# One core of a hybrid decoder layer: values computed in feature layout and transposed, an earlier query tile, and denominators in two fp32r parts

## The chip, the core and the metric

The kernel runs on one core of one Trainium2 chip. The metric is the device time of one execution in microseconds (us), and lower is better. In this kernel TensorE (PE in the profile) does the matrix products. ScalarE (ACT) and VectorE (DVE) carry results out of PSUM and do the elementwise work. GpSimd (POOL) splits every weight tile into two parts, and the SyncE queue (SP) loads the weights.

## What is computed

One layer over 528 tokens (16 meta tokens and a sequence of 512), model width 1024. One input projection feeds three parallel mixers (GLA, a sparse attention, mLSTM), whose outputs are gated and summed, and an MLP follows. The change concerns the values of GLA and of mLSTM (four heads of 256 columns each), the normaliser of mLSTM, and the first products of the sparse attention's query path.

```python
z = xn @ p["w_in"] + p["b_in"]          # 528 x 1024 times 1024 x N_COLS
# GLA, per chunk:   o = (q * exp(G)) @ S + A @ v
# mLSTM, per chunk:
num = w_inter[..., None] * jnp.einsum("bhtk,bhkv->bhtv", q, Cs) + jnp.einsum("bhts,bhsv->bhtv", P, v)
den = w_inter * jnp.einsum("bhtk,bhk->bht", q, ns) + jnp.sum(P, axis=-1)
h = num / jnp.maximum(jnp.abs(den), jnp.exp(-m))[..., None]
```

## The kernel before

**Precision.** Large products are made of three fp32r products: high part by high part, low by high, high by low. The input is held as `xh` and `xl`, features on partitions. SP loads a chunk of 1024 x 128 weights into `wraw`, and POOL writes its rounded part `whi` and the rest `wlo` (`hi_done` and `split_done` count them). Three raw and four split chunks are held.

**The stream of products.** `plan()` lists the tiles that TensorE computes in order. Each goes into one of two accumulators `GP[0]` and `GP[1]`, by turns. `gemm(name)` waits until its accumulator has been emptied (`gfree`) and its chunks are split, runs the tile's products and increments `gemm_done`. `evacuated(name)` waits until the result of a tile has been carried out. A tile of kind F (a feature tile) has 128 output features on partitions. With `both=True` it covers all 528 tokens in two halves of 264, so 8 x 3 x 2 = 48 products. The order on each engine is written out by hand, and an engine that waits holds back all that stands behind it.

**Values.** A head's values are needed with tokens on partitions. They are computed so: the input is the stationary operand and two weight chunks are streamed, 256 columns wide. Tiles `...A` and `...B` (kind V) take two token tiles of 128 each, 48 products a tile. A third tile `...M` (kinds VM and VT) computes 16 meta or last tokens, 16 products with 32 stationary columns (`xm`, L1879 and L1880). VectorE adds the bias from a broadcast row `vb` as it empties them (`values`, L1392 and L1397) into `vh` and `vm`.

**mLSTM, head h, on TensorE.** The query tile of the next head in two halves with `squares` between them, `scores` 0 and 1, the key tile, `scores` 2 and 3, values A of the next head, then `recalled` (the weighted values, L2291 and L2292). Then the denominators: sums of the weights over keys, by a matrix of ones in fp32, in two products of 112 and 400 columns (L2322, L2324). Then values B and M.

**mLSTM on the other engines.** VectorE multiplies the scores by decays (L1688), adds them up for the denominators (`weight_sums`, L1696 to L1700), runs the next head's two convolutions (`conv`, L1658 and L1660), and finishes the head. ScalarE runs the exponentials. After the last scores it takes one sigmoid for each convolution (L996), the output gate (L1039), loads the table for ln and exp (`lnexp`, L638), and squares the head's output (L1049).

```python
if more:
    conv_sig(h + 1, 1)
lnexp()
head_squares(h)
```

**The start.** The query path has two tiles, `cq0` and `cq1`, each computed in two halves of 256 tokens (`half`). TensorE begins with the high parts of `cq0`, as soon as two input tiles are there.

Of the kernel before, what the change touches and what calls it, by code (L numbers as in the profile page):

```python
# [24 lines left out]
D = 1024  # L25
# [44 lines left out]
def _rows():  # L70
    at = 0
    for name, n, src in [
        ("gq", 4, "b_in"), ("gk", 4, "b_in"), ("gr", 8, "b_in"), ("cq", 2, "b_in"), ("ckv", 1, "b_in"),
        ("ik", 1, "b_in"), ("mq", 4, "b_in"), ("mk", 4, "b_in"), ("mo", 8, "b_in"), ("gate", 24, "b_in"),
        ("a2", 4, "b_gla_a"), ("hg", 2, "g_gla_head"),
        ("hm", 2, "g_ml_head"), ("dq", 2, "g_dsa_q"), ("dkv", 1, "g_dsa_kv"), ("ig", 1, "idx_ln_g"),
        ("ib", 1, "idx_ln_b"), ("fb", 1, "ml_f_bias"), ("cv", 32, "ml_conv"),
    ]:
        ROWS[name] = at
        ROW_LIST.append((name, n, src))  # L80
        at += n
    return at
# [6 lines left out]
JOINED = {"gq": 8, "cq": 3, "mq": 8}  # L89
FOLLOWS = ("gk", "ckv", "mk")  # L90
# [21 lines left out]
NROWDMA = 22  # L112
# [22 lines left out]
def plan():  # L135
# [27 lines left out]
    def values(name, c0):  # L163
        c = [chunk("w_in", c0, P), chunk("w_in", c0 + P, P)]
        assert c[0] % 2 == 0
        tile(name + "A", c, 0, kind="V", off=0)
        tile(name + "B", c, 0, kind="V", off=2)
        tile(name + "M", c, 2, kind="VT" if name[0] == "m" else "VM")

    def pad():  # L170
        if len(chunks) % 2:
            chunks.append(None)
# [8 lines left out]
    state["slot"] ^= 1  # L181
# [42 lines left out]
    def all_values(name, c0):  # L224
        pad()
        values(name, c0)

    gla(0)
    all_values("gv0", C_GV)
    for h in range(HEADS):  # L230
        if h + 1 < HEADS:
            gla(h + 1)
        else:
            gates("ta", C_GATE, 0, 2)
        pairs("gr", C_GR, h)
        if h + 1 < HEADS:
            all_values(f"gv{h + 1}", C_GV + (h + 1) * DV)
# [6 lines left out]
    all_values("mv0", C_MV)  # L244
    for h in range(HEADS):
        if h + 1 < HEADS:
            feature(f"mq{h + 1}", "w_in", C_MQ + (h + 1) * DK, both=True)
            feature(f"mk{h + 1}", "w_in", C_MK + (h + 1) * DK, both=True)
        else:
            gates("tc", C_GATE + 2 * D, 0, 2)  # L250
        if h + 1 < HEADS:
            all_values(f"mv{h + 1}", C_MV + (h + 1) * DV)
# [37 lines left out]
def build(nc, a, line, scratch, rows, out):  # L290
# [3 lines left out]
    with ctx:  # L294
# [6 lines left out]
        def region(offset, specs):  # L301
# [23 lines left out]
        xm = sb("xm", [P, KT, 2 * META], F32R)  # L325
# [44 lines left out]
        (sgate, gtmp, vb, qh, ATm, kh, vh, vm, AT, sqo, rso, on, km) = region(AO, [  # L370
            ("sgate", [P, 2, SEQ], FP32), ("gtmp", [P, 2, SEQ], FP32), ("vb", [P, D], FP32),
# [3 lines left out]
        BO = AO + (2 * SEQ * 2 + D + 2 * SEQ + 2 * ALL + 2 * QT * DV + 2 * DV + QT * SEQ + SEQ + 2 * SEQ + SEQ + 2 * SEQ + 2 * P) * 4  # L375
# [7 lines left out]
        (zc, cv, sgc, lf_, bcum_, M_, uT, uTt, fbias_, um_, Mb, Md, Wd, Mt, Wt, ATt, later_t) = region(BO, [  # L383
# [5 lines left out]
            ("later_t", [2 * META, META], FP32)])  # L389
        (onesr,) = region(BO + (6 * ALL + 4 * SEQ + 144) * 4, [("onesr", [P, P], F32R)])  # L390
        later = ATm
        (sqr,) = region(AO + (7 * SEQ + D + 2 * ALL + 2 * QT * DV + 2 * DV + QT * SEQ) * 4, [("sqr", [P, 2, SEQ], F32R)])
        (qg,) = region(AO + (4 * SEQ + D) * 4, [("qg", [P, 2, QT, P + P // 2], FP32)])
# [17 lines left out]
        def gate_store(m):  # L411

            return [vh[:, 0, 0:2, :].rearrange("p a b -> p (a b)"), vh[:, 0, 2:4, :].rearrange("p a b -> p (a b)"),
                    kh[:, 0, 0:SEQ], qh[:, 0, :], vb[:, 0:SEQ], vb[:, SEQ:D], AT[:, 0, :], AT[:, 1, :]][m]
# [61 lines left out]
        ld_v, zpad, cv_ok, cs_ok, qk_ok = sem("ld_v"), sem("zpad"), sem("cv_ok"), sem("cs_ok"), sem("qk_ok")  # L476
# [3 lines left out]
        xt_ok, ml_c = sem("xt_ok"), sem("ml_consts")  # L480
# [147 lines left out]
        def _(act):  # L628
# [41 lines left out]
            def input_high(t):  # L670

                if t == QT:
# [3 lines left out]
                    act.wait_ge(xh_ok, KT + 1)  # L676
                    nc.scalar.activation(xm[:, :, 0:META], xh[:, :, 0:META].bitcast(FP32), ACT.Copy).then_inc(xh_ok, 1)
# [21 lines left out]
            for k in range(2):  # L699
                nc.scalar.activation(cq[:, k, :], ready(f"cq{k}")[:, 0:SEQ], ACT.Identity, bias=cc("cq", k)).then_inc(gfree[tl[f"cq{k}"].slot], 1)  # L700
# [144 lines left out]
            act.dma_start(vb[:, :], a["b_in"][0:1, C_GV:C_GV + D].broadcast_to([P, D])).then_inc(ld_a, 16)  # L845
# [81 lines left out]

            gate_of(0)
            for h in range(HEADS):
                last = h == HEADS - 1  # L930
                level(h, 0)
                if h:
                    squared(h - 1)
                level(h, 1)
# [20 lines left out]
                off_out(h)  # L955
                sigmoids(h)
                if last:

                    whole("gv3M")
# [20 lines left out]
            act.dma_start(vb[:, :], a["b_in"][0:1, C_MV:C_MV + D].broadcast_to([P, D])).then_inc(ld_v, 16)  # L980
# [64 lines left out]
            fetch_maxima(0)  # L1045
            def head_squares(h):
# [10 lines left out]
            for h in range(HEADS):  # L1057
# [15 lines left out]
                floor_of(h)  # L1073
                if more:
# [10 lines left out]
                if not more:  # L1085
                    gate_in("tc", 16, 2)
                head_squares(h)
            gate_in("tc", 16, 3)
            whole("mv3M")
# [88 lines left out]
        def _(dve):  # L1178
# [45 lines left out]
            def input_low(t):  # L1224
                if t == QT:
# [3 lines left out]
                    dve.wait_ge(xl_ok, KT + 1)  # L1229
                    nc.vector.tensor_copy(xm[:, :, META:2 * META], xl[:, :, 0:META].bitcast(FP32)).then_inc(xl_ok, 1)  # L1230
# [155 lines left out]
            dve.wait_ge(ld_a, 48)  # L1386

            def values(name, h, part):
                if part < 2:
                    t = tl[f"{name}{h}{'AB'[part]}"]  # L1390
                    ps = ready(f"{name}{h}{'AB'[part]}")
                    tt(vh[:, h % 2, 2 * part:2 * part + 2, :], ps[:, 0:2 * DV].rearrange("p (t n) -> p t n", t=2),  # L1392
                       vb[:, h * DV:(h + 1) * DV].unsqueeze(1).broadcast_to([P, 2, DV]), ALU.add).then_inc(gfree[t.slot], 1)
                    return
                ps = ready(f"{name}{h}M")
                dve.wait_ge(f16_ok, 2)
                stt(vm[0:2 * META, h % 2, :], vb[0:2 * META, h * DV:(h + 1) * DV], first16[:, :], ps[0:2 * META, 0:DV], ALU.mult, ALU.add).then_inc(gfree[tl[f"{name}{h}M"].slot], 1)  # L1397
# [91 lines left out]
            def off(h):  # L1489
# [6 lines left out]
                if h + 1 < HEADS:  # L1496
                    values("gv", h + 1, 0)
# [55 lines left out]
            for part in range(3):  # L1553
                values("gv", 0, part)
            for h in range(HEADS):
# [33 lines left out]
                if more:  # L1589
                    values("gv", h + 1, 1)  # L1590
                    values("gv", h + 1, 2)
# [5 lines left out]
            def gate_rows_of(m):  # L1597
# [18 lines left out]
                if m == 3:  # L1616
                    dve.wait_ge(gemm_done, tl["gv3M"].val)
                    nc.vector.tensor_copy(xm[:, :, 0:META], xh[:, :, SEQ:ALL].bitcast(FP32)).then_inc(xt_ok, 1)
                    nc.vector.tensor_copy(xm[:, :, META:2 * META], xl[:, :, SEQ:ALL].bitcast(FP32)).then_inc(xt_ok, 1)
# [4 lines left out]
                if m == 5:  # L1624
                    nc.vector.tensor_copy(later[:, 0:DIAG[0]], later_bigT[:, META:P])
# [75 lines left out]

            def denominator(h):
# [25 lines left out]
            dve.wait_ge(ld_v, 16)  # L1728
            for part in range(3):
                values("mv", 0, part)  # L1730
            for h in range(HEADS):
                more = h + 1 < HEADS
                masked(h)
                if h:
                    head_scaled(h - 1)
                for j in range(2):
# [6 lines left out]
                if more:  # L1743
                    conv(h + 1, 0)
                if h:
                    low_parts(8, h - 1)
                if more:
                    conv_mul(h + 1, 0)
                    conv(h + 1, 1)
                    values("mv", h + 1, 0)  # L1750
# [3 lines left out]
                if more:  # L1754
                    for part in range(1, 3):
                        values("mv", h + 1, part)
# [84 lines left out]
        def _(pe):  # L1841
# [9 lines left out]
            def gemm(name, part=None):  # L1851
# [22 lines left out]
                elif t.kind in ("V", "VM", "VT"):  # L1874
                    s0 = chunks[t.chunks[0]]["hl"]
                    if t.kind != "V":
                        for k in range(KT):
                            w = slice(k * P, (k + 1) * P)
                            mm(ps[0:2 * META, 0:DV], xm[:, k, :], whi[:, s0:s0 + 2, w], start=(k == 0), stop=False)  # L1879
                            ins = mm(ps[0:2 * META, 0:DV], xm[:, k, :], wlo[:, s0:s0 + 2, w], start=False, stop=(k == KT - 1))  # L1880
                    tokens = [] if t.kind != "V" else [0, 1] if part is None else [part]
                    first = 0 if name[0] == "m" else META
                    for i in tokens:
                        tok = slice(first + (t.off + i) * P, first + (t.off + i + 1) * P)
                        o_ = ps[:, i * DV:(i + 1) * DV]
                        for k in range(KT):
                            for p_, (at_, wt) in enumerate([(xh, whi), (xh, wlo), (xl, whi)]):
                                ins = mm(o_, at_[:, k, tok], wt[:, s0:s0 + 2, k * P:(k + 1) * P],  # L1888
# [564 lines left out]
```

## Time and profile before

| what | value |
|---|---|
| time, median of 3 runs | 1264.04 us (1263.27 to 1264.69) |
| the profiled execution, its time | 1264.5 us |
| its span in the trace | 1261.8 us |
| PE busy | 1253.5 us, 99% |
| POOL, DVE, ACT busy | 772.8, 629.2, 392.9 us |
| chain that ended last | PE 99% |

The chain that ended last is followed back from the last instruction. Here nearly all of it is TensorE's own work, one product behind the other. Matmuls are pipelined, so a row shows longer durations than what a product costs in a stream. The cost is the distance from one start to the next.

### The profile page before, as it was taken

Reading aid. Unit: us, or ns where it says so; the run is one execution under the profiler, and the core shown is the slowest. Engines: PE = TensorE matmul, PEld = TensorE weight load, DVE = VectorE, ACT = ScalarE, POOL = GpSimd, SP = SyncE. Lnnn points to the kernel's source line nnn. Section 1 sums busy time; section 2 is a strip of 40 time slices with the busy share of each in tenths; the row PEclk is TensorE's granted clock in tenths of the full one; section 3 lists DMA queues with packets and bytes.
Section 4 is the critical chain, followed back from the end, with each engine's and each line's share of the span. In section 5 each row is a group of like instructions: output and inputs, shape, how many; then the busy total and the mean of one; then the engine's idle time right before and its main releaser. Section 6 shows DMA issues by size and latency. Waiting matters only on the chain.

```text
span 1261.8 us, 17439 instructions
## 1 busy us (share of the span) xinstructions
PE 1253.5 (99%) x6561; PEld 1029.2 (82%) x6564; DVE 629.2 (50%) x1115; ACT 392.9 (31%) x810; POOL 772.8 (61%) x914
## 2 busy tenths in 40 slices
PE   9999999999999999999999999999999999999998
PEld 8866887677899899888899987887888888888886
DVE  4368888642276886835447773342511112333434
ACT  5343565533023323333024343312511111221322
POOL 8746430125584753758775556784876677888882
PEclk9999999999999999999999999999999999999999
DMA  7847200223231322322433333522233333232321
GB/s 177 241 122 224 68 1 26 68 67 94 71 97 51 84 62 56 84 68 84 117 110 78 86 97 100 188 95 84 84 101 100 85 100 105 96 100 84 101 84 67
DMA packets 167433, 120.08 MB, mean 95 GB/s; under 512 B 11367, under 2 KB 145613, under 8 KB 167350
## 3 DMA queue, kind: packets, MB, share of 16 engines
q1 hardware_dynamic: 160612, 107.79, 29.7%
q10 hardware_dynamic: 6738, 11.18, 2.7%
q8 instruction: 52, 0.85, 0.3%
q14 instruction: 31, 0.25, 0.1%
HBM read 114.71 MB, written 9.62 MB: 99 GB/s over the span
## 4 chain that ended last, share of the span: by engine, by line
PE 99%; DVE 0%; ACT 0%; issue 0%; DVEq 0%; ACTq 0%
PE GP L1873 46%; PE GP L1909 9%; PE PA L1909 9%; PE GP L1888 7%; PE GP L1870 6%; PE PA L2073 3%; PE GP L2135 3%; PE PA L2173 1%; PE PA L2110 1%; PE PA L2291 1%; PE GP L2366 1%; PE GP L1954 1%; PE PA L2043 1%; PE PA L2283 1%; PE PA L2074 1%; PE GP L1880 1%
## 5 line engine op out<-in xcount | busy, mean ns | idle before, releaser
L623 POOL TENSOR_TENSOR wlo<-wraw,whi 128x256 fp32r<-128x256 f32 x708 | 564.7, 828 | 14.7
L619 POOL TENSOR_SCALAR whi<-wraw 128x1024 fp32r<-128x1024 f32 x177 | 201.1, 1136 | 449.9 <-PE GP L1873 227.2
L1873 PE MATMUL GP<-xh,whi 128*128 128x512 f32 x352 | 144.8, 411 | 0.0
L1873 PE MATMUL GP<-xh,wlo 128*128 128x512 f32 x352 | 139.1, 395 | 0.0
L1873 PE MATMUL GP<-xl,whi 128*128 128x512 f32 x352 | 138.8, 394 | 0.0
L1815 DVE TENSOR_TENSOR ul<-U,uh 128x512 fp32r<-128x512 f32 x64 | 65.2, 1054 | 109.5 <-ACT uh L1157 109.5
L1873 PE MATMUL GP<-nh,whi 128*128 128x512 f32 x240 | 95.1, 396 | 0.0
L1873 PE MATMUL GP<-nl,whi 128*128 128x512 f32 x240 | 95.1, 396 | 0.0
L1873 PE MATMUL GP<-nh,wlo 128*128 128x512 f32 x240 | 95.1, 396 | 0.0
L1819 DVE SCALAR_TENSOR_TENSOR U<-GP,rrow 128x512 f32<-128x512 f32 x32 | 22.1, 692 | 141.7 <-PE GP L1873 140.3
L1873 PEld LDWEIGHTS GP<-xh,whi 128*128 128x128 f32 x352 | 66.2, 188 | 16.0 <-issue 1.5
L1873 PEld LDWEIGHTS GP<-xh,wlo 128*128 128x128 f32 x352 | 66.1, 188 | 15.2
L1873 PEld LDWEIGHTS GP<-xl,whi 128*128 128x128 f32 x352 | 66.3, 188 | 14.3 <-issue 0.5
L1157 ACT ACTIVATE uh<-U 128x512 fp32r<-128x512 f32 x64 | 37.2, 625 | 129.0 <-PE PA L1909 70.4
L1873 PE MATMUL GP<-yh,whi 128*128 128x512 f32 x192 | 76.3, 397 | 0.0
L1873 PE MATMUL GP<-yl,whi 128*128 128x512 f32 x192 | 76.1, 396 | 0.0
L1873 PE MATMUL GP<-yh,wlo 128*128 128x512 f32 x192 | 76.1, 396 | 0.0
L1888 PE MATMUL GP<-whi,xh 128*128 128x256 f32 x256 | 74.6, 292 | 0.2 <-DVE kh L1403 0.2
L1888 PE MATMUL GP<-wlo,xh 128*128 128x256 f32 x256 | 71.9, 281 | 0.0
L1888 PE MATMUL GP<-whi,xl 128*128 128x256 f32 x256 | 71.7, 280 | 0.0
L1161 ACT ACTIVATE U<-U 128x512 f32<-128x512 f32 x32 | 20.2, 632 | 152.9 <-DVE U L1819 152.9
L1873 PEld LDWEIGHTS GP<-nh,wlo 128*128 128x128 f32 x240 | 45.2, 188 | 11.0
(426 smaller groups left out, 2771.5 us busy)
## 6 DMA issues: line engine op xcount, KB each, us to landing
wraw<-in_w_in SPq DMA_DIRECT2D x75, 512.0 KB, 3.9
wraw<-in_w_up SPq DMA_DIRECT2D x32, 512.0 KB, 4.0
wraw<-in_w_down SPq DMA_DIRECT2D x32, 512.0 KB, 3.5
line_rows<-bias_line SPq DMA_DIRECT2D x8, 655.0 KB, 5.1
table<-line_rows SPq DMA_DIRECT2D x4, 1024.0 KB, 5.6
wraw<-in_w_br_dsa SPq DMA_DIRECT2D x8, 512.0 KB, 4.2
wraw<-in_w_br_gla SPq DMA_DIRECT2D x8, 512.0 KB, 3.9
wraw<-in_w_br_ml SPq DMA_DIRECT2D x8, 512.0 KB, 4.0
```

The lines of the kernel that those rows point to most:

```text
L619: nc.gpsimd.tensor_scalar(hi, src, 1.0, 1.0, ALU.mult, ALU.mult).then_inc(hi_done, 1)
L623: part = nc.gpsimd.tensor_tensor(lo[:, at:to], src[:, at:to], hi[:, at:to].bitcast(FP32), ALU.subtract)
L1157: nc.scalar.activation(uh[:, k % 4, :], U[:, k % FT, :], ACT.Copy).then_inc(uh_ok, 1)
L1161: nc.scalar.activation(U[:, m, :], U[:, m, :], ACT.Square).then_inc(U_ok, 1)
L1815: tt(ul[:, k % 4, :], U[:, k % FT, :], uh[:, k % 4, :].bitcast(FP32), ALU.subtract).then_inc(ul_ok, 1)
L1819: stt(U[:, m, :], ps[:, 0:SEQ], 0.0, rrow[:, :], ALU.max, ALU.mult).then_inc(gfree[tl[f"up{m}"].slot], 1)
L1870: ins = mm(ps[0:t.m, b * SEQ:b * SEQ + HALF], wt[:, s0, w], hx[:, k, b * HALF:(b + 1) * HALF], start=st, stop=sp_)
L1873: ins = mm(ps[0:t.m, 0:SEQ], wt[:, s0, w], av, start=st, stop=sp_)
L1888: ins = mm(o_, at_[:, k, tok], wt[:, s0:s0 + 2, k * P:(k + 1) * P], start=(k == 0 and p_ == 0), stop=(k == KT - 1 and p_ == 2))
L1909: ins = mm(accumulators(name, hf, i), av[:, i * P:(i + 1) * P], wt[:, c["hl"], k * SEQ:(k + 1) * SEQ], start=(n == 0 and k == 0 and p_ == ...
L2073: mm(bank(v % 2)[0:r, 0:w], qlat[:, h, TILE_AT[i]:TILE_AT[i + 1]], kvT[:, 0:w], start=True, stop=False)
L2135: ins = mm(pairs_of(o_, g), kvn[:, j, :], pairs_of(PT[:, g % 2, j, :], g), start=(j == 0), stop=(j == i))
```

## The change

Values become feature tiles. A head has two (`gv00`, `gv01`; `mv00`, `mv01`), each of 48 products of 264 columns, like keys. ScalarE empties such a tile into `vT` with the bias added (`value_in`). A new tile of kind T (`...T0`, `...T1`) then transposes `vT` on TensorE against the identity: four transposes of 128 tokens and one of 16. VectorE copies it to `vh` and `vm`; T1 of GLA goes by ScalarE (`values_copied`). The tiles M, the buffer `xm` and the broadcast rows `vb` go. The bias rows are loaded with the other rows (22 loads become 20). `cq1`'s first high half is issued before `cq0`'s second half, in the second bank of the same accumulator. The mLSTM denominators are rounded by ScalarE (`sum_hi`), the rest is taken by VectorE (`weight_rest`, `sum_lo`), and TensorE sums both by two fp32r products of 512 columns.

```diff
+    def value(name, c0, h, v):
+        feature(f"{name}{h}{v}", "w_in", c0 + (2 * h + v) * P, both=True)
+            def value_in(name, h, v):
+                if h:
+                    act.wait_ge(gemm_done, tl[f"{name}{h - 1}T{v}"].val)
+                t = tl[f"{name}{h}{v}"]
+                nc.scalar.activation(two(vT[:, v, :]), halves(ready(f"{name}{h}{v}")), ACT.Identity,
+                                     bias=cc(name, 2 * h + v)).then_inc(gfree[t.slot], 1)
...
@@ ScalarE, head h of mLSTM
                 floor_of(h)
+                act.wait_ge(sum_w, h + 1)
+                for c, s_ in WSUM:
+                    ins = nc.scalar.activation(Wr[:, 1, c], s_[:, c], ACT.Copy)
+                ins.then_inc(sum_hi, 1)
...
                 if more:
                     conv_sig(h + 1, 1)
                 lnexp()
-                if not more:
+                if more:
+                    value_in("mv", h + 1, 0)
+                else:
                     gate_in("tc", 16, 2)
                 head_squares(h)
+                if more:
+                    value_in("mv", h + 1, 1)
...
@@ VectorE
+            def weight_rest(h):
+                dve.wait_ge(sum_hi, h + 1)
+                for c, s_ in WSUM:
+                    ins = tt(Wr[:, 0, c], s_[:, c], Wr[:, 1, c].bitcast(FP32), ALU.subtract)
+                ins.then_inc(sum_lo, 1)
...
                 weight_sums(h)
                 if more:
                     conv(h + 1, 0)
+                weight_rest(h)
...
@@ TensorE
+                elif t.kind == "T":
+                    v, first = int(name[4]), 0 if name[0] == "m" else META
+                    few = slice(SEQ, ALL) if name[0] == "m" else slice(0, META)
+                    evacuated(name[0:3] + name[4])
+                    for i in range(QT):
+                        nc.tensor.transpose(ps[:, i * P:(i + 1) * P], vT[:, v, first + i * P:first + (i + 1) * P], ident[:, :])
+                    ins = nc.tensor.transpose(ps[0:META, SEQ:SEQ + P], vT[:, v, few], ident[:, :])
...
-                nxt("mvA")
+                nxt("mv0")
...
-                mm(bank(3)[:, 0:FROM[1]], ones[:, :], AT[:, 0, 0:FROM[1]], start=True, stop=True)
-                pe.wait_ge(sum_w, h + 1)
-                mm(bank(3)[:, FROM[1]:SEQ], ones[:, :], Wd[:, 0, FROM[1]:SEQ], start=True, stop=True).then_inc(av_ps, 1)
-                nxt("mvB")
-                nxt("mvM")
+                pe.wait_ge(sum_lo, h + 1)
+                mm(bank(3), onesr[:, :], Wr[:, 1, :], start=True, stop=False)
+                mm(bank(3), onesr[:, :], Wr[:, 0, :], start=False, stop=True).then_inc(av_ps, 1)
+                nxt("mvT0")
+                nxt("mv1")
...
@@ TensorE, start
             half("cq0", 0, low, False, True)
+            pe.wait_ge(hi_done, 2)
+            half("cq1", 0, high, True, False)
             pe.wait_ge(xl_ok, KT)
             half("cq0", 1, high, True, False)
```

TensorE at the end of mLSTM's head 0, before: the last of the weighted values, the denominators, and the first products of values B of head 1.

```order
L2291 MATMUL PA<-AT,vh 128x144
L2292 MATMUL PA<-ATt,vm 128x16
L2322 MATMUL PA<-AT,ones 128x112
L2324 MATMUL PA<-Wd,ones 128x400
L1888 MATMUL GP<-whi,xh 128x256
L1888 MATMUL GP<-wlo,xh 128x256
```

And now:

```order
L2305 MATMUL PA<-AT,vh 128x144
L2306 MATMUL PA<-ATt,vm 128x16
L2338 MATMUL PA<-Wd_r,onesr 128x512
L2339 MATMUL PA<-Wd_r,onesr 128x512
L1901 MATMUL GP<-ident,vT 128x128 x4
L1902 MATMUL GP<-ident,vT 16x128
L1892 MATMUL GP<-xh,whi 128x264 x2
```

The tile `mv1T0` (`ident,vT`) stands between the denominators and the next large tile, where products of the large tile followed at once.

ScalarE at the same place, before: the two sigmoids of head 1's convolutions (`sgc`), the output gate, the table load, the squares of head 0.

```order
L996 ACTIVATE sgc<-cv 128x528
L988 ACTIVATE zc<-GP,col 128x528
L1039 ACTIVATE sgate<-sgate 128x512 x2
L996 ACTIVATE sgc<-cv 128x528
L638 ACT_TABLE_LOAD
L1049 ACTIVATE sqo<-PA 128x1024
L1051 ACTIVATE gtmp<-gtmp 128x512
```

And now:

```order
L1018 ACTIVATE sgc<-cv 128x528
L1010 ACTIVATE zc<-GP,col 128x528
L1061 ACTIVATE sgate<-sgate 128x512 x2
L1018 ACTIVATE sgc<-cv 128x528
L645 ACT_TABLE_LOAD
L937 ACTIVATE vT<-GP,col 128x528
L1073 ACTIVATE sqo<-PA 128x1024
L1075 ACTIVATE gtmp<-gtmp 128x512
L937 ACTIVATE vT<-GP,col 128x528
```

The copy `vT` that `mv1T0` transposes is made behind the second sigmoid and the table load; the second copy follows the squares.

## Rows read from the trace of the kernel before

**Rows 1.** The page, busy time of TensorE, and its granted clock in 40 slices.
```profile
PE 1253.5 (99%) x6561; PEld 1029.2 (82%) x6564; DVE 629.2 (50%) x1115; ACT 392.9 (31%) x810; POOL 772.8 (61%) x914
...
PEclk9999999999999999999999999999999999999999
```

**Rows 2.** Waits of TensorE: releaser, us in total, times, longest us.
```profile
PE GP L1954 <- DVE xl L1235: 0.6, 1, 0.6
```

**Rows 3.** Instructions of L1888, window 340 to 375 us: duration min/median/max, first and last start.
```profile
L1888 PE MATMUL GP<-whi,xh x32: 279/280/387, 347.5 to 358.5; 128*128 128x256 f32 x32
```

**Rows 4.** Timeline of TensorE, tile M of GLA's head 0: start, us, line.
```profile
358.89 0.28 PE L1879 MATMUL GP<-whi,xm 128*32 128x256 f32 x1
...
360.73 0.40 PE L1873 MATMUL GP<-xh,whi 128*128 128x512 f32 x1
```

**Rows 5.** Timeline of TensorE, first half of a query tile in mLSTM, then `squares`.
```profile
680.94 0.40 PE L1870 MATMUL GP<-xh,whi 128*128 128x264 f32 x2
...
683.85 0.40 PE L2195 MATMUL PA<-sqr,onesr 128*128 128x512 f32 x1
...
684.32 0.40 PE L1870 MATMUL GP<-xh,whi 128*128 128x264 f32 x2
```

**Rows 6.** Timeline of TensorE, four transposes between fp32r products, GLA's head 0.
```profile
395.62 0.28 PE L1888 MATMUL GP<-whi,xl 128*128 128x256 f32 x1
...
395.88 0.30 PE L2235 MATMUL PA<-ident,km 128*128 128x128 f32 x1
...
396.02 0.49 PE L2237 MATMUL PA<-ident,KHt 128*128 128x128 f32 x3
...
396.27 0.36 PE L1888 MATMUL GP<-whi,xh 128*128 128x256 f32 x1
```

**Rows 7.** Timeline of TensorE, mLSTM's head 1 from its last scores to values B.
```profile
695.43 0.36 PE L1888 MATMUL GP<-whi,xh 128*128 128x256 f32 x1
...
701.17 0.59 PE L2291 MATMUL PA<-AT,vh 128*128 128x512 f32 x1
...
706.00 0.45 PE L2322 MATMUL PA<-AT,ones 128*128 128x112 f32 x2
...
707.10 0.28 PE L1888 MATMUL GP<-wlo,xh 128*128 128x256 f32 x1
```

**Rows 8.** Timeline of VectorE in the same stretch.
```profile
696.03 0.58 DVE L1696 TENSOR_TENSOR Wd<-AT 128x400 f32<-128x400 f32 x1
...
698.30 0.59 DVE L1700 TENSOR_TENSOR Wd<-Wd,ATt 16x16 f32<-16x16 f32 x1
...
699.33 2.74 DVE L1660 SCALAR_TENSOR_TENSOR cv<-zc,col,cv 128x528 f32<-128x528 f32 x3
```

**Rows 9.** Timeline of ScalarE in the same stretch.
```profile
702.66 0.68 ACT L988 ACTIVATE zc<-GP,col 128x528 f32<-128x528 f32 x1
...
706.95 0.65 ACT L996 ACTIVATE sgc<-cv 128x528 f32<-128x528 f32 x1 [2.58 <-DVE cv L1660]
707.62 1.28 ACT L638 ACT_TABLE_LOAD   x1
708.91 1.03 ACT L1049 ACTIVATE sqo<-PA 128x1024 f32<-128x1024 f32 x1
```

**Rows 10.** Timeline at the end of head 0: denominators on TensorE, table load on ScalarE.
```profile
672.45 0.45 PE L2322 MATMUL PA<-AT,ones 128*128 128x112 f32 x2
...
673.65 1.28 ACT L638 ACT_TABLE_LOAD   x1
```

**Rows 11.** Timeline of ScalarE in GLA, from the off-diagonal copies to the next head.
```profile
396.55 0.60 ACT L879 ACTIVATE AT<-PA 128x512 f32<-128x512 f32 x1 [5.85 <-PE PA L2237]
...
399.63 1.28 ACT L638 ACT_TABLE_LOAD   x1
```

**Rows 12.** Timeline of weight loads at the start, before the first real products.
```profile
1.24 4.90 PEld L1930 LDWEIGHTS PA<-ones 128*128 128x128 f32 x26 [1.24 <-DVE ones L1202]
...
7.89 0.86 PEld L1930 LDWEIGHTS PA<-ones 128*128 128x128 f32 x7 [0.24 <-issue]
```

More of the change, by code:

```diff
@@ L161, in feature, with turned @@
         tile(name, [c], 1, kind="F", m=m, kt=kt, both=both, rhs=rhs, off=0, width=m)
[L163 to L172, printed above, removed]
+    def turned(name, v):
+        tile(f"{name}T{v}", [], 0, kind="T")
     feature("cq0", "w_in", C_CQ)
+    state["slot"] = 0
     feature("cq1", "w_in", C_CQ + P)
+    tiles["cq1"].need = 0
     feature("ik", "w_in", None, both=True)
@@ L222, in gates @@
             feature(f"{name}{m}", "w_in", c0 + m * P)
-    def all_values(name, c0):
-        pad()
-        values(name, c0)
+    def value(name, c0, h, v):
+        feature(f"{name}{h}{v}", "w_in", c0 + (2 * h + v) * P, both=True)
     gla(0)
-    all_values("gv0", C_GV)
+    value("gv", C_GV, 0, 0)
+    value("gv", C_GV, 0, 1)
+    turned("gv0", 0)
+    turned("gv0", 1)
     for h in range(HEADS):
@@ L699, in _ @@
             for k in range(2):
-                nc.scalar.activation(cq[:, k, :], ready(f"cq{k}")[:, 0:SEQ], ACT.Identity, bias=cc("cq", k)).then_inc(gfree[tl[f"cq{k}"].slot], 1)
+                nc.scalar.activation(cq[:, k, :], ready(f"cq{k}")[:, k * SEQ:(k + 1) * SEQ], ACT.Identity, bias=cc("cq", k)).then_inc(gfree[tl[f"cq{k}"].slot], 1)
             whole("cq0")
@@ L955, in _ @@
                 off_out(h)
+                if not last:
+                    value_in("gv", h + 1, 0)
                 sigmoids(h)
+                if not last:
+                    value_in("gv", h + 1, 1)
                 if last:
-                    whole("gv3M")
                     gate_in("ta", 0, 3)
@@ L1084, in _ @@
                 lnexp()
-                if not more:
+                if more:
+                    value_in("mv", h + 1, 0)
+                else:
                     gate_in("tc", 16, 2)
                 head_squares(h)
+                if more:
+                    value_in("mv", h + 1, 1)
             gate_in("tc", 16, 3)
-            whole("mv3M")
             gate_in("tc", 16, 4)
@@ L1385, in _, with values @@
             nc.vector.tensor_copy(small[0:32, HALF:ALL], small[96:P, HALF:ALL]).then_inc(gla_c, 1)
[L1386 to L1397, printed above, removed]
+            def values(name, h, v):
+                ps, c = ready(f"{name}{h}T{v}"), slice(v * P, (v + 1) * P)
+                nc.vector.tensor_copy(vh[:, h % 2, :, c], ps[:, 0:SEQ].rearrange("p (t n) -> p t n", t=QT))
+                nc.vector.tensor_copy(vm[0:META, h % 2, c], ps[0:META, SEQ:SEQ + P]).then_inc(gfree[tl[f"{name}{h}T{v}"].slot], 1)
             def q_in(h):
@@ L1552, in _ @@
             forget_sums(0)
-            for part in range(3):
-                values("gv", 0, part)
+            values("gv", 0, 0)
             for h in range(HEADS):
@@ L1727, in _ @@
             dve.wait_ge(ml_c, 2)
-            dve.wait_ge(ld_v, 16)
-            for part in range(3):
-                values("mv", 0, part)
+            values("mv", 0, 0)
             for h in range(HEADS):
@@ L1735, in _ @@
                     head_scaled(h - 1)
+                values("mv", h, 1)
                 for j in range(2):
@@ L1754, in _ @@
                 if more:
-                    for part in range(1, 3):
-                        values("mv", h + 1, part)
+                    values("mv", h + 1, 0)
             head_scaled(HEADS - 1)
@@ L1873, in gemm @@
                                 ins = mm(ps[0:t.m, 0:SEQ], wt[:, s0, w], av, start=st, stop=sp_)
[L1874 to L1888, printed above, removed]
-                                         start=(k == 0 and p_ == 0), stop=(k == KT - 1 and p_ == 2))
+                elif t.kind == "T":
[5 more added lines that the diff above has]
+                    ins = nc.tensor.transpose(ps[0:META, SEQ:SEQ + P], vT[:, v, few], ident[:, :])
                 else:
@@ L1988, in _ @@
             ins.then_inc(xt_ps, 1)
-            pe.wait_ge(hi_done, 2)
-            half("cq1", 0, high, True, False)
             half("cq1", 1, high, False, False)
@@ L2268, in _ @@
             gemm("mk0")
-            for nm in ("mv0A", "mv0B"):
+            for nm in ("mv00", "mv01", "mv0T0"):
                 gemm(nm)
-            pe.wait_ge(xt_ok, 2)
-            gemm("mv0M")
             pe.wait_ge(M_ok, 1)
```

112 lines of the change are left out of this document (61 added, 51 removed).

## The prediction

> **What bounds the kernel now.** I read the page first. TensorE is busy for 1253.5 of 1261.8 us and its granted clock is 9 tenths or more in each of 40 slices [rows 1], so no stretch leaves TensorE waiting for long, and the chain that ended last is TensorE. The list of its waits then tells how thin the rest is: the one wait that this change touches is 0.6 us for the low part of the input [rows 2]. A change to such a kernel has two prices. What it takes from or adds to TensorE's own stream counts in full. And each result that a product now needs from another engine must be there when TensorE arrives, since no idle time exists to absorb it. So I price the products by the distance of their starts, and then follow the three engines at each new wait.
>
> **TensorE's stream.** Eight heads (four of GLA, four of mLSTM) change their values.
> (a) Tile M goes: 16 products from 358.89 to the next tile at 360.73, 1.84 us [rows 4]. Eight times: -14.7 us.
> (b) The 96 large products of a head stay 96, but stream 264 columns for 256. L1888 shows 32 of every third product from 347.5 to 358.5, which is 11.0 us for 93 products, 0.1183 each [rows 3]. The 24 products of a half query tile take 680.94 to 683.85, 0.1213 each [rows 5]. 768 x 0.0030 = +2.3 us.
> (c) Ten transposes a head, in 16 tiles of five. In the trace four stand between products: the product at 395.62 would have been followed at 395.74, and the next came at 396.27 [rows 6]. So four cost 0.53 us with the change of kind, five 0.66. Where a neighbour is fp32 already (the weighted values of GLA, the scores) the change of kind is paid before, so I take 0.60 a tile, 16 tiles: +9.6 us. Bounds: three transposes alone take 396.02 to 396.27, so five take at least 0.42 (6.7 us in all), and at most 0.72 (11.5).
> (d) The denominators: from 706.00 to where the stream is regular again, 707.10 less one step of 0.12, is 0.98 us [rows 7]. Two fp32r products of 512 columns with ones are in the trace, 683.85 to 684.32, 0.47 us [rows 5]. Four heads: -2.0 us.
> (e) The start: `cq1`'s 16 high products fill the wait of 0.6 us for `xl` [rows 2]. Their weights come second from the split, and nothing waits behind them for longer. -0.6 us.
> The stream's sum is -5.4 us. The loads of the bias rows lie beside other work and cost nothing.
>
> **The new waits.** A T tile needs `vT` from ScalarE, so each of the 16 has to be checked.
> GLA, T0: ScalarE is free behind the copy at 396.55, so from about 397.2 [rows 11], and the first value tile is ready by then. The product at 396.27 begins a half of the second value tile [rows 6]; with the other half that is 48 x 0.1213 = 5.8 us, so TensorE comes to T0 after 402. No wait. T1: ScalarE is done with the sigmoids and the load at 400.9 [rows 11], waits for the second value tile and copies it while TensorE runs T0 and the weighted values. No wait. Only in the first head does T1 come directly behind T0, and likewise mLSTM's first query tile behind `mv0T0`: each copy of 0.7 us is covered by 0.6 us of transposes, which leaves 0.2 us or so each, +0.4 us.
> mLSTM, T1: it comes after a whole query tile. No wait.
> mLSTM, T0 of heads 1, 2 and 3 is the place that decides. TensorE comes to it directly behind the denominators, but ScalarE makes its input behind the second convolution's sigmoid and the table load. I follow head 1 of the trace, where T0 of head 2 will stand.
> TensorE: the value tile begins at 695.43 and takes 5.82 now, the weighted values take 701.17 to 706.00, 4.83, the denominators 0.47 [rows 7]. It arrives at 706.55.
> ScalarE: the sigmoid at 706.95 waits for VectorE's `cv` [rows 9]. VectorE's chain begins with the last scores just before 695.43 and runs without a gap (the sums end at 698.9, the first convolution at 702.07 [rows 8]), and the change puts `weight_rest` into it: 400 columns by 0.58 [rows 8], 112 columns by about 0.25, together 0.83. So the sigmoid begins at 707.78, the load 0.67 later, the copy 1.29 after that (706.95, 707.62, 708.91 in rows 9) at 709.74. The copy of 128x528 from PSUM is 0.68 [rows 9], its signal some 0.1: T0 can begin at 710.5. TensorE stands for 3.9 us.
> Head 2 of the trace repeats head 1, 33.55 us later, so T0 of head 3 waits 3.9 too. In head 0 the table load stands at 673.65, and the denominators began at 672.45 [rows 10]. There VectorE had to wait 0.7 us for the first sigmoid, so `weight_rest` hides in it but for 0.1: copy from 675.05, T0 from 675.8. TensorE arrives at 672.45 + 0.09 + 0.47 = 673.0, and waits 2.8 us.
> Together 10.6 us. These can't be recovered later in the head: T0 must be emptied and the next tile computed before the scores, and the scores restart the same chain, so the wait comes back in each head.
> What else is new on ScalarE, the two rounding copies, lies in a gap: the sums end at 698.9, the copies need 0.3 and 0.6, the table load 1.28, and the first sigmoid is due at 702.1 when its convolution ends. `weight_rest` ends near 702.9, and the denominators need it at 706.1, so 3.2 us are left.
>
> **A rule and a row.** Behind the load at 707.62 the next activation starts at 708.91, and before it the sigmoid of 0.65 begins at 706.95, so the switch costs 1.29 us and nothing else fits in [rows 9]. The Trainium skill (ScalarE: Activation LUTs, What ACT_TABLE_LOAD costs) adds a drain of some 1380 ns to each load. By that, T0 would be 1.4 us later in three heads and the sum would be 4.1 us higher; the row decides against it.
>
> **The sum.** -5.4 + 0.4 + 10.6 = +5.6 us on a span of 1261.8 us, so 1267.4. The profiled execution took 1264.5 us, 0.5 above the median, so I work from the median of 1264.04: 1269.7 us, +0.44%.
>
> **Rivals.**
> *The copy is in time* (faster). If ScalarE had `vT` by 706.5, the waits would vanish, and 1264.04 - 5.4 + 0.4 = 1259.0 us stays. It turns at 3.9 us: the sigmoid would have to start at 703.9 and not 707.8. For it: VectorE's other work in the head gets less (its bias additions go). Against it: those stood behind the convolutions or before the scores, and the sigmoid's wait is for `cv` itself [rows 9].
> *The wait is cut to a half*, if the convolution starts earlier or the stream before T0 is longer than I priced it: 1262 to 1266 us.
> *The clock falls in the waits.* The granted clock stays full through the trace [rows 1], but the only wait of TensorE inside the work that is listed here is 0.6 us long [rows 2], and waits of 3.9 us are new. The first loads of all, after idle time, come every 0.19 us (26 in 4.90), later ones of the same form every 0.12 (7 in 0.86) [rows 12], though the granted clock of that slice shows nothing of it. If TensorE wakes up so behind a wait, with the clock at 1.2 for a while and not at 2.4 GHz, the price is about what the start paid: 26 x 0.065 = 1.7 us a wait. In two or three heads that gives 1273.1 to 1274.8. The Trainium skill (TensorE: Matmul & The Clock Gate, HAM oscillation) says that idle gaps between bursts of products bring the slow clock back. No row here has such a gap, so this stays a rival with a chance of 0.22.
> *Another new wait*, as `sum_lo` coming late or T1 of GLA held by ScalarE's queue: 3.2 us of slack would have to go; a few us, 1272 to 1275.
>
> **How the numbers follow.** Forecast as summed 0.58, clock 0.22, another wait 0.05, cut wait 0.07, copy in time 0.08. Bounds of the forecast alone: transposes -2.9 to +1.9, `weight_rest` and the copy together 0.3 less or 0.5 more in each of three heads, 264 columns 1 us either way: 1266.3 to 1273. To hold 8 in 10 it needs part of the clock case and no faster one: 1265.5 to 1274.5. No change is within 0.2% (2.5 us, about what a measurement of this kernel tells from none), 1261.5 to 1266.6. Faster 0.09, same 0.06, slower 0.85.
>
> **What the changed profile would show.** Waits of TensorE for ScalarE's `vT` at the transposes, three times, 2.8, 3.9 and 3.9 us, and the sum of its idle time up by 10 us. No rows of `xm`; 80 transposes of `vT` at 0.60 us per five. The two denominator products 0.47 us apart from start to T0's earliest place. A wait at `xl` of under 0.1 us at the start. `sum_lo` not among TensorE's waits. The granted clock below 1 behind a wait would speak for the clock. Wrong it would be if `cv` is ready some 3 us earlier relative to the last scores, or if T0 waits nowhere.

## The result and the profile after

The changed kernel takes 1282.33 us (median of 4 runs, 1282.08 to 1282.79) against 1263.76 us for the kernel before (4 runs, 1263.27 to 1264.69). The ratio is 1.0145, 95% interval 1.0132 to 1.0158: slower by 18.6 us. The forecast was slower by 5.6, 1269.7 us, with a range up to 1274.5. The direction is right and the size is not.

The profiled span is 1280.9 us, 19.1 more than before. This is the page of the changed kernel, which answers to [rows 1]; the second line is TensorE's busy share in tenths, the third its granted clock.

```profile
PE 1255.3 (98%) x6505; PEld 1031.0 (80%) x6508; DVE 621.5 (49%) x1120; ACT 408.1 (32%) x841; POOL 773.9 (60%) x914
...
PE   9999999999999999999998889999999999999998
...
PEclk9999999999999999999998889999999999999999
```

Three slices, 672 to 769 us, are below 9 in both rows; T0 of mLSTM's heads 1, 2 and 3 lies in them. The list of TensorE's waits says for what (releaser, us in total, times, longest us); `xl` of [rows 2] is gone from it.

```profile
PE GP L1901 <- ACT vT L937: 17.4, 4, 6.2
...
PE GP L1892 <- ACT vT L937: 0.4, 1, 0.4
```

L1901 is the transpose, L937 ScalarE's copy. Of the 17.4 us, 0.34 is T1 of GLA's first head. The rest is T0 of mLSTM's heads 1, 2 and 3: 4.62, 6.21 and 6.19 us. TensorE's timeline (start, us, line), first the transposes of `mv0T1`, then head 2, to compare with [rows 7]:

```profile
652.04 0.60 PE L1901 MATMUL GP<-ident,vT 128*128 128x128 f32 x4
...
711.41 0.48 PE L2338 MATMUL PA<-Wd_r,onesr 128*128 128x512 f32 x1
711.73 0.39 PE L2339 MATMUL PA<-Wd_r,onesr 128*128 128x512 f32 x1
718.32 1.09 PE L1901 MATMUL GP<-ident,vT 128*128 128x128 f32 x4 [6.21 <-ACT vT L937]
...
729.74 0.40 PE L2209 MATMUL PA<-sqr,onesr 128*128 128x512 f32 x1
```

The wait stands at the place that the prediction named. Two things are off. It is 6.2 us and not 3.9. And the transposes take 1.09 us for four, where four took 0.60 at 652.04: the clock is low. ScalarE there, the rows that answer to [rows 9]:

```profile
715.52 0.64 ACT L1018 ACTIVATE sgc<-cv 128x528 f32<-128x528 f32 x1 [5.92 <-DVE cv L1677]
716.18 1.28 ACT L645 ACT_TABLE_LOAD   x1
717.48 0.70 ACT L937 ACTIVATE vT<-GP,col 128x528 f32<-128x528 f32 x1
```

Sigmoid, load, copy follow each other as worked out, 1.96 us from the first start to the third. It is the sigmoid that starts late, and it waits for VectorE. VectorE's rows, for [rows 8], and below them GpSimd's:

```profile
707.21 1.11 DVE L1723 TENSOR_TENSOR Wd_r<-AT,Wd_r 128x112 fp32r<-128x112 f32 x1
708.24 0.56 DVE L1723 TENSOR_TENSOR Wd_r<-Wd,Wd_r 128x400 fp32r<-128x400 f32 x1
708.73 2.35 DVE L1562 TENSOR_TENSOR yl<-on,yh 128x512 fp32r<-128x512 f32 x2
711.00 1.21 DVE L1688 SCALAR_TENSOR_TENSOR qh<-cv,sgc 128x512 f32<-128x512 f32 x1
712.34 0.74 DVE L1675 TENSOR_SCALAR cv<-zc,col 128x528 f32<-128x528 f32 x1
713.11 2.38 DVE L1677 SCALAR_TENSOR_TENSOR cv<-zc,col,cv 128x528 f32<-128x528 f32 x3
```

```profile
706.91 1.29 POOL L626 TENSOR_SCALAR whi<-wraw 128x1024 fp32r<-128x1024 f32 x1 [1.78 <-PE GP L1892]
708.28 4.50 POOL L630 TENSOR_TENSOR wlo<-wraw,whi 128x256 fp32r<-128x256 f32 x4
```

112 columns take 1.11 us and 400 columns 0.56. All that is slow begins before 712.8, while GpSimd splits a weight chunk. In the kernel before GpSimd did nothing in this stretch: both value chunks were held until tile M (L1880) was done. Its row there, with the idle time ahead of it:

```profile
714.82 1.86 POOL L619 TENSOR_SCALAR whi<-wraw 128x1024 fp32r<-128x1024 f32 x1 [14.92 <-PE GP L1880]
```

Now a chunk ends with its own tile.

The granted clock and the load of the DMA engines in the same stretch, by windows (busy us and count for PE, PEld, DVE, ACT and POOL, then the granted clock, DMA share, GB/s):

```profile
709.00:711.00 2.00, 2.00 (x7) 1.18 (x8) 2.00 (x3) 0.60 (x2) 2.00 (x3) 1.00 0.01 4
713.00:715.00 2.00, 0.00 (x0) 0.00 (x0) 1.89 (x4) 0.00 (x0) 0.00 (x0) 1.00 0.48 104
715.00:717.00 2.00, 0.00 (x0) 0.00 (x0) 1.26 (x3) 1.46 (x2) 0.00 (x0) 0.76 0.53 158
717.00:719.00 2.00, 0.68 (x4) 0.71 (x5) 1.41 (x3) 1.99 (x4) 0.00 (x0) 0.50 0.00 0
719.00:721.00 2.00, 2.00 (x11) 1.92 (x11) 1.81 (x3) 0.61 (x2) 0.00 (x0) 0.50 0.00 0
721.00:723.00 2.00, 2.00 (x11) 2.00 (x11) 1.97 (x5) 0.00 (x0) 0.00 (x0) 0.53 0.00 0
723.00:725.00 2.00, 2.00 (x19) 2.00 (x18) 0.20 (x2) 0.00 (x0) 0.00 (x0) 1.00 0.00 0
```

TensorE is idle from 712 to 718.3, its clock falls to 0.50, the 1.2 GHz level, and comes back after 722. A window of 2 us touches 11 products at the low level and 19 at the full one. DMA is not what slows VectorE: from 709 to 711, where two steps of `yl` take 2.35 us, it moves 4 GB/s.

From these rows came the theory for the experiments: -5.4 us of stream as forecast, +17.8 us of waits, and +6 to 7 us of work at the low clock, together +19. The rivals are named with each run.

### The profile page after: what moved, and what is told of

Same layout as the page of the kernel before. It is cut to its first block, busy times and chain, and to the rows that moved or that the text cites. A ratio compares the mean times of both kernels' runs of the same rounds, so it can differ in the third digit from the quotient of the medians.

```text
span 1280.9 us, 17359 instructions
## 1 busy us (share of the span) xinstructions
PE 1255.3 (98%) x6505; PEld 1031.0 (80%) x6508; DVE 621.5 (49%) x1120; ACT 408.1 (32%) x841; POOL 773.9 (60%) x914
## 4 chain that ended last, share of the span: by engine, by line
PE 94%; DVE 3%; ACT 1%; issue 1%; POOL 1%; DVEq 0%; ACTq 0%; POOLq 0%
PE GP L1895 45%; PE GP L1892 13%; PE GP L1922 9%; PE PA L1922 9%; PE PA L2087 3%; PE GP L2149 3%; PE PA L2187 1%; PE PA L2124 1%; DVE cv L1677 1%; PE GP L2381 1%; PE GP L1968 1%; PE PA L2057 1%; PE PA L2297 1%; PE GP L1901 1%; PE PA L2088 1%
## 5 line engine op out<-in xcount | busy, mean ns | idle before, releaser
L630 POOL TENSOR_TENSOR wlo<-wraw,whi 128x256 fp32r<-128x256 f32 x708 | 577.7, 846 | 14.8
L626 POOL TENSOR_SCALAR whi<-wraw 128x1024 fp32r<-128x1024 f32 x177 | 188.7, 1066 | 467.9 <-PE GP L1895 248.1
L1892 PE MATMUL GP<-xh,whi 128*128 128x264 f32 x480 | 104.3, 299 | 0.7 <-ACT vT L937 0.4
L1892 PE MATMUL GP<-xl,whi 128*128 128x264 f32 x480 | 99.3, 289 | 0.0
L1892 PE MATMUL GP<-xh,wlo 128*128 128x264 f32 x480 | 98.8, 288 | 0.0
L1892 PEld LDWEIGHTS GP<-xh,whi 128*128 128x128 f32 x480 | 77.5, 194 | 4.5 <-issue 2.1
L1895 PEld LDWEIGHTS GP<-xh,whi 128*128 128x128 f32 x352 | 66.2, 188 | 16.6 <-issue 1.9
L1895 PEld LDWEIGHTS GP<-xh,wlo 128*128 128x128 f32 x352 | 66.1, 188 | 15.5
L1895 PEld LDWEIGHTS GP<-xl,whi 128*128 128x128 f32 x352 | 66.3, 188 | 14.1 <-issue 0.5
L1892 PEld LDWEIGHTS GP<-xl,whi 128*128 128x128 f32 x480 | 76.6, 193 | 0.0
L1892 PEld LDWEIGHTS GP<-xh,wlo 128*128 128x128 f32 x480 | 76.2, 193 | 0.0
```

Source lines behind the costliest of these rows:

```text
L626: nc.gpsimd.tensor_scalar(hi, src, 1.0, 1.0, ALU.mult, ALU.mult).then_inc(hi_done, 1)
L630: part = nc.gpsimd.tensor_tensor(lo[:, at:to], src[:, at:to], hi[:, at:to].bitcast(FP32), ALU.subtract)
L1892: ins = mm(ps[0:t.m, b * SEQ:b * SEQ + HALF], wt[:, s0, w], hx[:, k, b * HALF:(b + 1) * HALF], start=st, stop=sp_)
L1895: ins = mm(ps[0:t.m, 0:SEQ], wt[:, s0, w], av, start=st, stop=sp_)
```

## First experiments: the wait, its length, the clock, the denominators

All are edits of the changed kernel. The kernel before took 1263.64 us beside them (7 runs).

**The copy earlier.** ScalarE's queue is the nearest suspect: the copy stands behind a sigmoid that waits.

```diff
                     conv_in(h + 1, 1)
+                    value_in("mv", h + 1, 0)
...
                 lnexp()
-                if more:
-                    value_in("mv", h + 1, 0)
-                else:
+                if not more:
```

> The changed kernel, but ScalarE makes the copy vT of the next head's first value tile right behind the copy of its key tile (conv_in), ahead of the output gate, the second sigmoid and the table load; nothing else moves. Theory from the trace of the changed kernel: its excess of 19 us over the kernel before is -5.4 us of stream, +17.8 us of waits for vT (4.6, 6.2 and 6.2 at T0 of heads 1 to 3, 0.4 twice at the first heads) and +6 to 7 us of slow clock behind the three long waits. Then the three long waits go and with them the slow clock: 1264.0 - 5.4 + 0.8 = 1259.4 us, up to 1262 if the keys of the next head (kh, km) are now late where they were not. Rival, the copy is late for another reason than the queue behind the sigmoid and the load (ScalarE itself is full, or the accumulator is): the waits stay within 1 us of what they are, 1281 to 1283 us. Rival, the waits go but the clock stays low, since something else than the wait brings it down: 1265 to 1267 us.

It took 1278.99 us, ratio 1.012 (1.0105 to 1.0135). None of the three cases came. The long waits at T0 are gone, yet almost all the time stays. The waits of this kernel:

```profile
PE GP L1891 <- DVE vm L1419: 8.1, 2, 5.2
PE GP L1894 <- DVE vm L1419: 5.2, 1, 5.2
```

L1891 and L1894 are the large products of the tile behind `mv1`: the next query tile, or the gate tile in the last head. It goes into the accumulator that T0 has filled, and VectorE empties that in `values`, behind the denominator and the sums of squares. TensorE passes T0 on time and stands one tile later, 2.8, 5.2 and 5.2 us. The clock falls again (0.50 from 718 to 724). So a tile of kind T has two dependencies one behind the other, input and emptying, and both hung on VectorE's chain. My theory was incomplete, and the theory that the head follows VectorE's chain was not in my list.

**GpSimd idle beside the chain.** The chunk of the first value tile is held until the second is computed.

```diff
             value("mv", C_MV, h + 1, 1)
+            chunks[tiles[f"mv{h + 1}0"].chunks[0]]["end"] = tiles[f"mv{h + 1}1"].val
```

> The changed kernel, but the weight chunk of the first value tile of mLSTM's heads 1 to 3 counts as used until the second value tile is computed, as two chunks were held before; so GpSimd has no chunk to split while VectorE runs the convolutions. Theory: VectorE's instructions in the chain to T0 take longer beside GpSimd's split (a copy for the low part 1.11 us against an estimate of 0.58 from its neighbour of the same size, qh 1.2 us against 0.7, yl 2.35 us for two against 1.3), and this makes the waits at T0 4.6, 6.2 and 6.2 us where 2.8, 3.9 and 3.9 were worked out. With GpSimd idle there these three come to 3 to 4.5 us each, 5 to 7 us less in sum, and the slow clock behind them stays: 1275.5 to 1278 us. Rival, the VectorE instructions are slow for themselves (their operands, their addresses): no change, 1282 us within 1 us. Rival, the later split makes a weight tile late: a new wait of TensorE for wlo, over 1282 us.

It took 1273.83 us, ratio 1.008 (1.0065 to 1.0095): 8.5 us less than the changed kernel. The expected 1275.5 to 1278 was too high, and the direction and the cause are those of the theory. VectorE's rows at the same place, TensorE's wait, and GpSimd, idle for 18.5 us until 720.01:

```profile
703.57 0.27 DVE L1724 TENSOR_TENSOR Wd_r<-AT,Wd_r 128x112 fp32r<-128x112 f32 x1
703.76 0.57 DVE L1724 TENSOR_TENSOR Wd_r<-Wd,Wd_r 128x400 fp32r<-128x400 f32 x1
704.24 1.28 DVE L1563 TENSOR_TENSOR yl<-on,yh 128x512 fp32r<-128x512 f32 x2
705.45 0.68 DVE L1689 SCALAR_TENSOR_TENSOR qh<-cv,sgc 128x512 f32<-128x512 f32 x1
706.26 0.49 DVE L1676 TENSOR_SCALAR cv<-zc,col 128x528 f32<-128x528 f32 x1
706.79 2.38 DVE L1678 SCALAR_TENSOR_TENSOR cv<-zc,col,cv 128x528 f32<-128x528 f32 x3
...
712.00 1.09 PE L1902 MATMUL GP<-ident,vT 128*128 128x128 f32 x4 [3.53 <-ACT vT L938]
...
720.01 1.04 POOL L627 TENSOR_SCALAR whi<-wraw 128x1024 fp32r<-128x1024 f32 x1 [18.53 <-PE GP L1893]
```

From `weight_rest` to the last three steps of the convolution it is 3.22 us here (703.57 to 706.79) and 5.90 in the changed kernel (707.21 to 713.11). The difference, 2.68 us, is that of the waits, 6.21 and 3.53, to the hundredth. From 703.6 to 706.8 DMA moves 151 GB/s here, and the steps of `yl` take 1.28 us all the same. The three waits are now 2.44, 3.53 and 3.51 us; I had worked out 2.8, 3.9 and 3.9.

**The wait filled.** TensorE gets products that nobody reads, ahead of T0.

```diff
+                for _ in range((18, 24, 24, 0)[h]):
+                    mm(bank(2), onesr[:, :], xh[:, 0, 0:SEQ], start=True, stop=True)
                 nxt("mvT0")
```

> The changed kernel with products that nobody reads put between the denominators and T0 in heads 0, 1 and 2: 18, 24 and 24 fp32r products of 512 columns with ones, 4.2 to 4.3 and 5.7 us at full clock, which lie in the waits of 4.6, 6.2 and 6.2 us. Theory, the wait brings the granted clock down to 0.50 and the work behind it then runs at that clock for some microseconds: with TensorE at work through the wait the clock stays at 1.0, T0 begins as late as before, and the three stretches behind it take 2.3, 2.1 and 1.8 us less, 1276 us within 1. Rival, those stretches are slow for another reason than the clock, or the clock falls whether TensorE works or not: 1282 us within 1. Rival, the filling work itself makes T0 late: over 1283 us.

It took 1276.56 us, ratio 1.0098 (1.0082 to 1.0115): 5.8 us less, with useless work added. TensorE's rows and two windows of this kernel:

```profile
710.76 4.83 PE L2341 MATMUL PA<-xh,onesr 128*128 128x512 f32 x20
716.22 0.63 PE L1901 MATMUL GP<-ident,vT 128*128 128x128 f32 x4 [0.63 <-ACT vT L937]
...
725.55 0.40 PE L2209 MATMUL PA<-sqr,onesr 128*128 128x512 f32 x1
...
718.00:724.00 6.00, 6.00 (x52) 6.00 (x51) 3.03 (x7) 1.11 (x4) 1.04 (x1) 1.00 0.01 3
724.00:730.00 6.00, 6.00 (x48) 5.65 (x47) 1.73 (x3) 3.22 (x7) 3.56 (x6) 1.00 0.49 123
```

The view begins within the 24 products, so its first row counts 20 of them. From T0 to `squares` it takes 9.33 us (716.22 to 725.55) at full clock, and in the changed kernel 11.42 (718.32 to 729.74). The wait itself is not shortened; what the wait does to the clock costs 2.1 us here and 5.8 over three heads.

**The old denominators.**

```diff
-                pe.wait_ge(sum_lo, h + 1)
-                mm(bank(3), onesr[:, :], Wr[:, 1, :], start=True, stop=False)
-                mm(bank(3), onesr[:, :], Wr[:, 0, :], start=False, stop=True).then_inc(av_ps, 1)
+                mm(bank(3)[:, 0:FROM[1]], ones[:, :], AT[:, 0, 0:FROM[1]], start=True, stop=True)
+                pe.wait_ge(sum_w, h + 1)
+                mm(bank(3)[:, FROM[1]:SEQ], ones[:, :], Wd[:, 0, FROM[1]:SEQ], start=True, stop=True).then_inc(av_ps, 1)
```

> The changed kernel with its denominators as before: two fp32 products of 112 and 400 columns, no rounding copies on ScalarE, no weight_rest on VectorE. Theory: weight_rest stands in the chain to the waits at T0, and takes 1.67 us there (1.11 and 0.56), not the 0.83 us that I had priced. Then T0 begins 1.7 us earlier in two heads and about 1 us earlier in the first, and only in the last head, which has no such wait, the dearer products cost 0.5 us: 1282.3 - 1.7 - 1.7 - 1.0 + 0.5 = 1278.4 us. By the prediction's own prices (0.83 in two heads, 0.1 in one): 1281.0 us. Rival, the denominators save 2 us in TensorE's stream and weight_rest costs nothing: 1284.3 us.

It took 1278.99 us, ratio 1.0123 (1.0105 to 1.0142), near the 1278.4 of the theory. Its four runs lie from 1277.4 to 1282.2, and its interval overlaps that of the changed kernel (1.0132 to 1.0158), so the size is loose. The trace is that of the slowest run, 1282.16 us. The waits at T0 in it are 3.32, 4.92 and 4.92 us, 1.3 us shorter each. The dearer products take some 0.4 us of that, so the chain comes only 0.9 us earlier and not 1.7. VectorE's rows in it:

```profile
706.65 2.66 DVE L1558 TENSOR_TENSOR yl<-on,yh 128x512 fp32r<-128x512 f32 x2
...
711.36 2.72 DVE L1673 SCALAR_TENSOR_TENSOR cv<-zc,col,cv 128x528 f32<-128x528 f32 x3
```

These were 2.35 and 2.38 us in the changed kernel. What moves up falls beside GpSimd's split in its turn (it ends at 711.9). By the medians, the part of the change that was to save 2 us costs 3.3 under these waits; that it costs anything is not clear of the spread of these runs.

## Second experiments: both ends of the transposed tile, and the forecast's own case

The kernel before took 1264.09 us beside these (21 runs).

**Copy and emptying early.** VectorE empties T0 where it waits for the sigmoid in any case.

```diff
                     conv(h + 1, 1)
+                    values("mv", h + 1, 0)
                     conv_mul(h + 1, 1)
                 denominator(h)
                 head_sums(h)
-                if more:
-                    values("mv", h + 1, 0)
```

> The early copy of the last call, and VectorE also empties T0 earlier: values of the next head stand between its second convolution and the product with the sigmoid, where it waits 0.7 us for ScalarE anyway, and not behind the denominator and the sums of squares. The early copy alone gave 1279.0 us, since TensorE did not wait at T0 any more but 2.8, 5.2 and 5.2 us at the next query tile for the accumulator that T0 had filled. Theory: a T tile has two waits in a row, its input from ScalarE and its emptying by VectorE, which stood behind the same chain; with both early the three long waits go. What is left is the sum of squares, which ends at 719.3 in the trace of the early copy while TensorE would come to it at 717.8: 1 to 2 us in two heads, with some slow clock. 1259.4 us if nothing is late, 1262 to 1266 with these waits. Rival, the head is bound by VectorE's chain as a whole, wherever the tile is emptied: then the waits move on once more and the time stays at 1275 to 1280 us.

It took 1264.36 us, ratio 1.0001 (0.9992 to 1.001): 14.6 us less than with the early copy alone, and in the range of the theory. The next limit is the one named:

```profile
PE PA L2207 <- DVE sqr L1739: 2.7, 2, 1.4
PE PA L2295 <- ACT rso L650: 1.3, 2, 0.8
```

**And the chunk held.** Both edits and that of the held chunk.

> Both early moves and the chunk held, so that GpSimd does not split beside VectorE's chain. Holding the chunk alone took 8.5 us from the changed kernel and brought the three waits to 2.4, 3.5 and 3.5 us. Theory: no wait is left but the two of 0.4 us at the first heads, the clock stays full, and the stream's -5.4 us come out: 1264.0 - 5.4 + 0.8 = 1259.4 us, within 1.5; faster than before by 0.3 to 0.4%. Rival, the stream's price is wrong (a transposed tile costs more than 0.60 us, 264 columns more than priced): 1261 to 1264 us with no waits in the trace. Rival, a wait for the sums of squares or for the accumulator is still there: over 1262 us, and the list of waits names it.

It took 1259.13 us (1258.57 to 1259.55, 5 runs), ratio 0.9962 (0.9948 to 0.9975). That is faster than the kernel before by 5.0 us, and by 23 than the kernel as changed. TensorE's clock row and its waits for `vT` in it:

```profile
PEclk9999999999999999999999999999999999999999
...
PE GP L1891 <- ACT vT L938: 0.4, 1, 0.4
PE GP L1900 <- ACT vT L938: 0.3, 1, 0.3
```

Its span is 1257.2 us, 4.6 below that of before, with 0.7 us of new waits in it: the stream is 5.3 us shorter. I had summed 5.4.

**The forecast's case.** The chunk held and the shorter waits filled (10, 14 and 14 products).

> The changed kernel with the chunk held and products that nobody reads in the waits at T0 (10, 14 and 14 fp32r products of 512 columns, 2.3 and 3.3 us of the 2.4 and 3.5 us). This is the case that I forecast: waits of the length worked out and no slow clock. Theory, the two excesses are independent: the chunk's hold gave 8.5 us, the filling alone 5.8 us on longer waits, so both give 1282.3 - 8.5 - 4 to 6 = 1268 to 1270 us, beside the forecast of 1269.7. Rival, most of the slow clock's price was already in the 8.5 us: 1272 to 1274 us.

It took 1268.53 us, ratio 1.0037 (1.0023 to 1.005). This is the kernel that I had forecast, waits of the length worked out and a full clock: forecast 1269.7. With the same waits left empty (the held chunk alone) it was 1273.83, which is what the rival of the clock had named, 1273.1 to 1274.8. So the slow clock costs 5.3 us over three waits even at the forecast's length.

**The denominators alone**, put into the kernel before (the same copies, differences and products as in the change, with two semaphores that this kernel already had).

> The kernel before with the change of the denominators alone: ScalarE's two rounding copies, weight_rest on VectorE, two fp32r products of 512 columns for two fp32 ones. Theory: TensorE's stream loses 0.5 us in each of four heads, and VectorE's chain, 0.7 to 0.8 us longer, has some 5 us of slack before the next head's scores: 1263.7 - 2.0 = 1261.7 us, within 0.5. Rival, weight_rest makes the keys or the sums of squares late and the gain goes: 1263.5 to 1265 us.

It took 1262.32 us, ratio 0.9988 (0.9979 to 0.9997), or -1.5 us by the ratio with an interval from -2.7 to -0.4. The -2.0 lies in it, and the rival of no gain does not.

## Why the prediction missed

The 18.6 us by their parts: -5.3 of stream (the fixed kernel), +0.8 at the first heads, +9.5 of waits at T0 with GpSimd idle beside the chain (trace with the chunk held), +7.5 more of them with GpSimd splitting (17.0 less 9.5), and +5.8 of slow clock (the filled kernel). Their sum is 18.3.

- *TensorE's stream, -5.4*: right in sum, in part by luck, since errors of single terms cancel. A T tile costs 0.46 us before a large tile (408.23 to 408.69) and 0.54 ahead of scores or weighted values (452.97 to 453.51), where I took 0.60 for all and expected the second kind to be the cheaper. So (c) is 8.0 us and not 9.6. The denominators gave 1.5 and not 2.0, within their interval. The start lost its wait, (e). In GLA's first head the 96 value products take 11.78 us (347.00 to 358.78) and took 11.44 (347.45 to 358.89), 0.34 more and not 0.29, or 2.7 us over eight heads for (b). With these values the terms sum to some -6.1, and the span shows -5.3; which term holds the other 0.8 us stays open.
- *The place of the new waits*: right. T0 of heads 1 to 3 and nowhere else but 0.4 us twice; `sum_lo` is not among the waits.
- *The length of the new waits, 10.6*: this is the step that failed first; they measured 17.0. "VectorE's chain ... runs without a gap, and the change puts `weight_rest` into it: ... together 0.83" priced the chain from rows of the kernel before, in which GpSimd stood idle. That was true of the trace and false of the changed kernel, because the change also frees a weight chunk one tile earlier. `weight_rest` then took 1.11 and 0.56 us, the next two low parts 2.35 for 1.28, `qh` 1.21 for 0.68. With GpSimd kept idle the same chain gave 9.5 us of waits and `weight_rest` 0.27 and 0.57, the 0.83 that was priced.
- *The clock*: this is the second step that failed. It was left out of the sum and priced at 1.7 us a wait, as a rival, with a chance of 0.22. It measured 1.9 (5.8 in three), and 1.8 with the shorter waits (5.3 in three). The size was right and the chance was not. I gave most of the weight to the sum without it, though no row showed a wait of this length without a slow clock behind it.
- *"These can't be recovered later in the head"*: true for the kernel as changed, but not complete. Had the copy been in time, the rival of 1259.0 us would still not have come. The emptying of T0 was the next wait, 13.3 us in three places, and I had not followed what T0's own result needs. The rival of 1259.0 was right only for three edits together, which gave 1259.1.
- *The range*: the bounds as listed, -2.9, three times -0.3 and -1 below, +1.9, three times +0.5 and +1 above, add up to 1264.9 to 1274.1 and not to 1266.3 to 1273. The time lies outside both.

The Trainium skill (SBUF — State Buffer, "SBUF: two separate sides") says that VectorE and GpSimd share one pair of ports, which goes for a whole instruction to the one that starts first, that a VectorE instruction with two SBUF inputs contends for it with a GpSimd instruction that reads SBUF, and that the DMA side does not. The trace agrees in its signs. The 112-column instruction started at 707.21, when GpSimd's `whi` (706.91 to 708.20) was under way, and ended at 708.32, 0.84 us later than alone. The 400-column one started at 708.24, just ahead of GpSimd's next at 708.28, and took no longer than alone (0.56 for 0.57). With GpSimd idle the last three steps of the convolution took 2.38 us in the changed kernel at 104 GB/s of DMA, and 2.38 with the chunk held at 0 GB/s. That the ports are the reason is argued from this timing; the runs show only that GpSimd's work beside the chain is. Had this been weighed against the freed chunk, the wait would have been priced longer.

The Trainium skill (TensorE: Matmul & The Clock Gate, "HAM oscillation") was cited for the rival of the clock, that idle gaps between bursts of products bring the slow clock back. The windows agree with it: 0.50 behind each of the three long waits (676 to 680, 717 to 721, 757 to 763).

## What to carry to other kernels

Durations taken from the trace of before hold only as long as the neighbour engine does what it did there: when a change frees a buffer earlier, look who starts to work on it, and beside whom. When a tile is put into a full stream, follow both its input and its emptying, each to the queue that holds it. And when TensorE gets a wait of some microseconds that it did not have, count the low clock behind it as part of the forecast: here it was a third as large as the waits.

## What the runs showed of the hardware

- Waits of 1.3 to 1.4 us (for `sqr`, twice) left the granted clock at 1.00 in the windows behind them, and the mean at 0.999. Behind the wait of 2.44 us, with the chunk held (it ends at 674.10), the clock was 0.72 from 672 to 676 us and 0.85 from 676 to 680, and 0.50 in each window of 1 us from 674 to 677. Between these two lengths nothing was measured.
- Behind a table load the next activation started at once (716.18 + 1.28 us, then 717.48), as in the kernel before.
- Products without a use, put into a wait, made the kernel faster by 5.8 us.
- VectorE beside GpSimd: +0.5 us for each instruction of 512 columns with two inputs in SBUF (1.21 for 0.68; 2.35 for two, 1.28 alone), and +0.25 even for one with a single input (0.74 for 0.49). None for the instruction of 400 columns that started ahead of GpSimd's.
